# S5 mixer of a hybrid decoder trunk: from a scan over 256 tokens to chunks of 8 tokens

## The reference, cut to what matters

```python
xr = jnp.einsum('blgh,gph->lbgp', ug, bbr)
xi = jnp.einsum('blgh,gph->lbgp', ug, bbi)
# h[t] = a * h[t-1] + x[t], complex, over the 256 positions
_, _, hr, hi = lax.associative_scan(_complex_linear_combine, (ar.., ai.., xr, xi), axis=0)
y = (jnp.einsum('lbgp,ghp->blgh', hr, c_re) - jnp.einsum('lbgp,ghp->blgh', hi, c_im) + d * ug)
y = jax.nn.gelu(y.reshape(bsz, seq, B_WIDTH))
y = y * jax.nn.sigmoid(y @ glu_w + glu_b)
```

## Time and profile before

| | us |
|---|---|
| median of 3 runs (lowest, highest) | 800.15 (800.11, 800.49) |
| profiled execution, its own time | 800.82 |
| its span | 798.8 |
| TensorE busy | 687.8 (86%) |
| VectorE busy | 524.1 (66%) |
| ScalarE busy | 362.2 (45%) |
| GpSimd busy | 316.4 (40%) |

### The profile page before, as it was taken

One profiled execution on the slowest core, in us unless ns is written; L12 is line 12 of the kernel. 1 busy time (PEld: TensorE's weight loads), 2 busy tenths in 40 slices (PEclk: granted clock), 3 DMA queues, 4 the chain that ended last, 5 costly groups with the idle time before them and its releaser, 6 DMA issues.

```text
span 798.8 us, 11006 instructions
## 1 busy us (share of the span) xinstructions
PE 687.8 (86%) x4020; PEld 606.3 (76%) x4020; DVE 524.1 (66%) x925; ACT 362.2 (45%) x656; POOL 316.4 (40%) x485
## 2 busy tenths in 40 slices
PE   2881944988989999999999697597998999999994
PEld 2771833976879999999978585476788999999983
DVE  5629999486385555666557999768447645555553
ACT  3550142366554454444436316155735544444441
POOL 5699993255305349999000444335510000000000
PEclk9995885799999999999999988689999999999998
DMA  9530310010168556556635350000125566666631
GB/s 258 172 105 0 111 52 1 1 53 27 54 185 246 196 186 185 167 184 201 210 108 169 105 163 1 1 27 27 54 89 166 167 203 191 187 185 188 186 127 80
DMA packets 51876, 100.25 MB, mean 126 GB/s; under 512 B 11093, under 2 KB 15902, under 8 KB 51822
## 3 DMA queue, kind: packets, MB, share of 16 engines
q1 hardware_dynamic: 48750, 96.40, 39.0%
q0 software_dynamic: 720, 1.97, 1.0%
q10 hardware_dynamic: 2352, 1.18, 0.6%
HBM read 98.48 MB, written 1.05 MB: 125 GB/s over the span
## 4 chain that ended last, share of the span: by engine, by line
PE 61%; DVE 25%; issue 6%; POOL 4%; ACT 2%; DMA 1%; DVEq 0%; SPq 0%; ACTq 0%; POOLq 0%
PE pb L1408 61%; DVE dtmp L978 6%; DVE w_lo L1051 4%; DVE scan L1119 2%; DVE dtmp L985 1%; DVE x L985 1%; DVE btab L1320 1%; POOL e L519 1%; DVE h_lo L985 1%; POOL bt L519 1%; DMA pos_i<-in_positions 1%; DVE top L1204 1%; DVE scan L978 1%; ACT btab L884 1%; DVE dtmp L1109 1%
## 5 line engine op out<-in xcount | busy, mean ns | idle before, releaser
L1051 DVE TENSOR_TENSOR w_lo<-raw,w_hi 128x1024 fp32r<-128x1024 f32 (+2 forms) x176 | 220.1, 1268 | 140.5 <-ACT w_hi L725 140.2
L725 ACT ACTIVATE w_hi<-raw 128x1024 fp32r<-128x1024 f32 (+2 forms) x184 | 188.2, 1028 | 255.0 <-PE pb L1408 255.0
L1408 PE MATMUL pb<-h_hi,w_hi 128*128 128x256 f32 x512 | 145.0, 283 | 1.8 <-DVE h_lo L985 1.8
L1408 PE MATMUL pb<-h_lo,w_hi 128*128 128x256 f32 x512 | 144.9, 283 | 0.0
L1408 PE MATMUL pb<-h_hi,w_lo 128*128 128x256 f32 x512 | 144.9, 283 | 0.0
L523 POOL TENSOR_SCALAR pst<-stat 128x2 f32<-128x2 f32 (+1 forms) x11 | 2.8, 255 | 307.5 <-ACT proj L729 278.7
L1408 PE MATMUL pb<-w_hi,h_hi 128*128 128x512 f32 (+2 forms) x224 | 86.0, 384 | 21.3 <-DVE w_lo L1051 20.4
L1408 PEld LDWEIGHTS pb<-h_hi,w_hi 128*128 128x128 f32 x512 | 98.2, 192 | 2.7 <-DVE w_lo L1051 2.2
L1408 PE MATMUL pb<-w_hi,z_hi 128*128 128x512 f32 x256 | 99.8, 390 | 0.0
L1408 PE MATMUL pb<-w_hi,z_lo 128*128 128x512 f32 x256 | 99.8, 390 | 0.0
L1408 PE MATMUL pb<-w_lo,z_hi 128*128 128x512 f32 x256 | 99.6, 389 | 0.0
(11 more groups left out here) (267 smaller groups left out, 1212.2 us busy)
## 6 DMA issues: line engine op xcount, KB each, us to landing
raw<-in_w_up SPq DMA_DIRECT2D x64, 512.0 KB, 3.8
raw<-in_w_down SPq DMA_DIRECT2D x64, 512.0 KB, 4.3
raw<-in_w_in SPq DMA_DIRECT2D x24, 512.0 KB, 4.6
raw<-in_w_out SPq DMA_DIRECT2D x16, 512.0 KB, 3.8
raw<-in_w_in SPq DMA_DIRECT2D x8, 308.0 KB, 3.1
raw<-in_w_in SPq DMA_DIRECT2D x8, 280.0 KB, 3.2
x<-in_x ACTq DMA_DIRECT2D x1, 1024.0 KB, 5.3
out<-x SPq DMA_DIRECT2D x2, 512.0 KB, 2.7
```

Source lines behind the costliest of these rows:

```text
L725: hi_made.by(act.activation(w_hi[:, n % RING, 0:width(n)], raw[:, n % RING, 0:width(n)], ACT.Copy))
L1051: lo_made.by(dve.tensor_tensor(w_lo[:, n % RING, 0:width(n)], raw[:, n % RING, 0:width(n)], w_hi[:, n % RING, 0:width(n)].bitcast(F32), AL ...
L1408: return pe.matmul(o, l, r, start=start, stop=stop, skip_group_check=True)
```

## The change

The sequence is cut into 32 chunks of 8 tokens, and a chunk's work becomes products.

- `uc`: eight transfers take u from rows of tokens to rows of chunks (SP, after piece 10), ScalarE reorders it, TensorE transposes it to `uu` (16 inputs times 8 tokens on the partitions, 32 chunks along them).
- `bp`: GpSimd forms B times a power of the state factor for each place in the chunk; 16 transposes give `sw`. `s5_sums`, 32 products, gives what each chunk adds to the states.
- `s5_states` on VectorE turns these by `rot`, runs one scan over 32 chunks of all eight pairs for each of the two parts, turns back, and writes the state at each chunk's start to `ez`.
- `s5_kernel`, 16 products of B with `ca` (C times a power), gives the response at lags 0 to 7. `s5_lags` adds the D term and copies to `rk`. SP writes `rk` to memory and reads it back in 16 transfers as the triangular blocks `tk`.
- `s5_out` is 16 products of `tk` with `uu` and 16 of `ca` with `ez`. The result has rows of channel and place in the chunk. After the GELU it is transposed (`y_back`), regrouped by eight transfers to `ytok`, and transposed again (`y_turned`) for the GLU product, which moves to unit 14; ScalarE's first two `split` parts move from units 15 and 17 to 17 and 18.
- The four rounds, `et`, `btab`, `ctab` and GpSimd's turning back are gone. C is loaded by SP for both layers and laid out by ScalarE (`c_table`), for layer 1 during layer 0.
- In layer 0 TensorE's first transposes wait for x itself instead of a mark of VectorE; VectorE clears `bd`, `ez` and `tk` at the start and sums `ident` to `m16`.

```diff
-ROUNDS = 4
+CQ = 8
+NC = SEQ // CQ
...
+                        if n == 11:
+                            sp.wait_ge(tile_sb.sem, tile_sb.at(L, 1))
+                            for t in range(TT):
+                                for q in range(4):
+                                    sp.dma_start(uc[32 * q + 16 * t:32 * q + 16 * t + 16],
+                                                 proj[:, t, O_U + 64 * q:O_U + 64 * q + 64]).then_inc(uc_in.sem, 16)
+                        if n == 16 and L < DEPTH - 1:
+                            sp.wait_ge(ct_ps.sem, ct_ps.at(L, 1))
+                            load_c(sp, L + 1)
...
+                        if n == 24:
+                            sp.wait_ge(rk_sb.sem, rk_sb.at(L, 1))
+                            sp.dma_start(rk_hbm[L], rk).then_inc(rk_out.sem, 16)
+                            sp.wait_ge(rk_out.sem, rk_out.at(L, 16))
+                            rows = rk_hbm[L].rearrange("(g i) j n -> i j g n", i=16)
+                            for s in range(CQ):
+                                for j in range(2):
+                                    sp.dma_start(tk[16 * s:16 * s + 16, 8 * j:8 * j + 8, s:CQ, :].rearrange("p g s o -> p g (s o)"),
+                                                 rows[:, j, :, 0:PART - 16 * s]).then_inc(tk_in.sem, 8 * 2)
+                        if n == 26:
+                            sp.wait_ge(yb_sb.sem, yb_sb.at(L, 1))
+                            for t in range(TT):
+                                for g in range(4):
+                                    sp.dma_start(ytok[:, t, 64 * g:64 * g + 64],
+                                                 yc[32 * g + 16 * t:32 * g + 16 * t + 16].rearrange("p s q o -> p s (q o)"))\
+                                        .then_inc(yt_in.sem, 16)
...
+                for g in range(2):
+                    m = pool.tensor_copy(bd[64 * g:64 * g + 64, :, :, g, :], bb[64 * g:64 * g + 64])
+                    if g == 0:
...
+                pool.wait_ge(prep_b.sem, prep_b.at(occ, 1))
...
+            def prep_inputs(occ):
...
+                step(pool.tensor_copy(pmag[:, :, 1], S(1)))
...
+                for n in (1, 2, 4):
+                    tt(pmag[:, :, n + 1:2 * n + 1], pmag[:, :, 1:n + 1],
+                       pmag[:, :, n:n + 1].to_broadcast([PART, PAIRS, n]), ALU.mult, False)
+                    step(double(pw, n, n))
+                for i in range(2):
+                    tt(pa[:, i], pw[:, i], pmag[:], ALU.mult, i == 1)
+                A = [pa[:, i, :, CQ:0:-1].unsqueeze(3).to_broadcast([PART, PAIRS, CQ, 16]) for i in range(2)]
+                B = [bb[:, i].unsqueeze(2).to_broadcast([PART, PAIRS, CQ, 16]) for i in range(2)]
+                prep_w.by(cmul(bp[:, :, 0], bp[:, :, 1], A[0], A[1], B[0], B[1], *W))
...
+            def prep_outputs(occ):
+                step(pool.tensor_copy(dec[:, :, 1:NC], pmag[:, :, CQ:CQ + 1].to_broadcast([PART, PAIRS, NC - 1])))
+                pool.wait_ge(prep_w.sem, prep_w.at(occ, 1))
...
                 for n in (1, 2, 4, 8):
...
+                    step(double(rot, n, n))
+                prep_r.by(double(rot, 16, 15))
+                pool.wait_ge(prep_r.sem, prep_r.at(occ, 1))
...
+                tt(ca[:, :, 0], A[0], B[0], ALU.mult, False)
+                tt(W[0], A[1], B[1], ALU.mult, False)
+                tt(ca[:, :, 1], A[0], B[1], ALU.mult, False)
+                tt(W[1], A[1], B[0], ALU.mult)
+                tt(ca[:, :, 0], ca[:, :, 0], W[0], ALU.add, False)
+                prep_c.by(pool.tensor_tensor(ca[:, :, 1], ca[:, :, 1], W[1], ALU.subtract))
...
-                for r in range(ROUNDS):
-                    pool.wait_ge(scanned.sem, scanned.at(L, r + 1))
...
+                if L == 0:
+                    prep_outputs(0)
...
+                    if n == 12:
+                        act.wait_ge(uc_in.sem, uc_in.at(L, 16 * 8))
+                        uc_sb.by(act.activation(up_.rearrange("p l (s h) -> p l s h", s=CQ),
+                                                uc.rearrange("p s (l h) -> p l s h", l=4), ACT.Copy))
+                act.wait_ge(u_ps.sem, u_ps.at(L, 1))
+                u_sb.by(act.activation(uu[:].rearrange("p (q l) c -> p l q c", l=4),
+                                       pb[0][:].rearrange("p (l q c) -> p l q c", l=4, q=4), ACT.Copy))
...
+                act.wait_ge(sw_ps.sem, sw_ps.at(L, 1))
+                for i, b in enumerate((1, 2, 3, 0)):
...
+                sw_sb.by(m)
...
-                    if i in (4, 6):
-                        transposed(6 + (i - 4) // 2)
+                    if i in (2, 5):
+                        transposed(6 + (i - 2) // 3)
...
+                    if i == 4:
+                        act.wait_ge(y_ps.sem, y_ps.at(L, 1))
+                        y_sq.by(act.activation(yt, pb[7][:], ACT.Square, scale=0.044715 ** 0.5))
+                    if i == 6:
...
+                    if i == 9:
+                        act.wait_ge(yb_ps.sem, yb_ps.at(L, 1))
+                        yb_sb.by(act.activation(yc.rearrange("p s q o -> p q s o"),
+                                                pb[7][:].rearrange("p (q s o) -> p q s o", q=4, s=CQ), ACT.Copy))
+                    if i == 13:
+                        act.wait_ge(yk_ps.sem, yk_ps.at(L, 1))
+                        yk_sb.by(act.activation(yg, pb[7][:], ACT.Copy))
...
+                def s5_states():
+                    dve.wait_ge(xs_ps.sem, xs_ps.at(L, 1))
+                    dve.wait_ge(prep_r.sem, prep_r.at(L, 1))
...
+                    tt(P[0], x2, c2, ALU.mult, False)
+                    xs_read.by(dve.tensor_tensor(P[1], x2, s2, ALU.mult))
...
+                    dve.wait_ge(xs_read.sem, xs_read.at(L, 1))
+                    tt(P[2][:, 0], P[0][:, 0], P[1][:, 1], ALU.add, False)
+                    tt(P[2][:, 1], P[0][:, 1], P[1][:, 0], ALU.subtract)
...
+                    for i in range(2):
+                        step(dve.tensor_tensor_scan(P[3][:, i], d, P[2][:, i], 0.0, ALU.mult, ALU.add), i == 1)
+                    tt(P[0], P[3], c2, ALU.mult, False)
+                    tt(P[1], P[3], s2, ALU.mult)
...
+                    for g in range(2):
...
+                        step(dve.tensor_tensor(ez[h, 0, :, g, 1:NC], Q[0][h, 0], Q[1][h, 1], ALU.subtract), False)
+                        m = dve.tensor_tensor(ez[h, 1, :, g, 1:NC], Q[1][h, 0], Q[0][h, 1], ALU.add)
...
+                    ez_made.by(m)
...
+                def s5_lags():
+                    dve.wait_ge(rk_ps.sem, rk_ps.at(L, 1))
...
+                    step(dve.tensor_copy(rk[:, :, 16:PART], src[:, :, 16:PART]), False)
...
+                        m = stt(rk[:, j, 0:16], m16[:], s5d[:, L, j:j + 1], src[:, j, 0:16], ALU.mult, ALU.add)
...
+                    rk_sb.by(m)
...
-                for n in range(12, 16):
+                for n in range(12, 20):
...
+                def u_transposed():
+                    pe.wait_ge(uc_sb.sem, uc_sb.at(L, 1))
+                    for g in range(4):
+                        m = pe.transpose(pb[0][:, g * PART:(g + 1) * PART], up_[:, g, :], ident[:])
+                    u_ps.by(m)
...
+                def s5_inputs():
+                    pe.wait_ge(prep_w.sem, prep_w.at(L, 1))
+                    pe.wait_ge(u_sb.sem, u_sb.at(L, 1))
+                    if L == 0:
+                        pe.wait_ge(ct_sb.sem, ct_sb.at(0, 1))
+                    for j in range(PAIRS):
+                        for i in range(2):
+                            b = (1, 2, 3, 0)[j // 2]
+                            m = pe.transpose(pb[b][:, (2 * (j % 2) + i) * PART:(2 * (j % 2) + i + 1) * PART],
+                                             bp[:, j, i].rearrange("p s h -> p (s h)"), ident[:])
+                    sw_ps.by(m)
...
+                def s5_sums():
+                    pe.wait_ge(sw_sb.sem, sw_sb.at(L, 1))
+                    for i in range(2):
+                        for j in range(PAIRS):
+                            for g in range(2):
+                                m = mm(pb[2][64 * g:64 * g + 64, i * SEQ + j * NC:i * SEQ + (j + 1) * NC],
+                                       sw[:, j, i, 64 * g:64 * g + 64], uu[:, 2 * j + g, :], (i, j) == (0, 0), True)
+                    xs_ps.by(m)
...
+                def s5_kernel():
+                    pe.wait_ge(prep_c.sem, prep_c.at(L, 1))
...
+                        for i in range(2):
+                            for jj in range(4):
+                                j = 4 * a + jj
+                                m = mm(pb[7][32 * jj:32 * jj + 32, a * PART:(a + 1) * PART],
+                                       bd[:, i, j].rearrange("p g h -> p (g h)"),
+                                       ca[:, j, i].rearrange("p s h -> p (s h)"), (a, i) == (0, 0), i == 1)
+                    rk_ps.by(m)
...
+                tile(1)
                 tile(2)
-                bu(1)
+                u_transposed()
+                s5_inputs()
```

(39 more changed lines are left out.)

372 lines of the change are left out of this document (158 added, 214 removed).

## The result

Measured: 764.64 us median (761.49 to 766.20, 4 runs) against 800.32 (800.11 to 801.12, 4 runs), a ratio of 0.9548 with the 95% interval 0.9516 to 0.9579. The profiled execution took 766.2, its span 764.5. The forecast was 755, so the kernel is 36 us faster where 45 were expected. The time was gained where it was looked for, and more of it than forecast; a good part was given back in the attention loop.

The account below looks back on a forecast made before the run. The chain was TensorE 61% and VectorE 25%, the latter in two pre-loop stretches. From 800.82: -32.7 (layer 0), -15.7 (layer 1), +4 (loops), -0.4 (start) gave 756.0, median 755; range 741 to 777.

Parts of the forecast that it names:

- The gate of layer 0: Layer 0 before the loop: GpSimd's prep_w becomes the gate, bp at 58.5 (55 to 63), tile 3 starting at 61.5.
- forecast 17.9: From the end of tile 4 to the loop start, VectorE sets the time and takes 17.9 us in each layer.
- s5_sums is ... 64 records: Before tile 4: 32 float32 products, two records each, priced from c_first and other short products at 7.0 us.
- The upper end, 7.5: Upper end of the forecast's range for s5_sums, 7.0 us, with 3.5 as the lower end.
- Rival C: s5_sums products run in pairs on overlapping column groups: 3.5 us less per layer, 748 in all; chance 0.13.
- priced cold (13.1): Layer 0 before the loop: tile 3 takes 13.1 us, as an earlier tile 3 that also restarted cold.
- 64 records of 0.117, 7.5: In the attention loop: s5_out takes 7.5 us against 9.1 before, a gain of 1.6 a layer.
- rival A: Short products don't get the upper clock: s5_out costs 7.5 us more a layer, 770 or 776; chance 0.20.
- Priced 0.9: In the loop: tk lands at T+12.0, TensorE reaches s5_out at T+11, so it waits 0.9 us.
- Rival B: Transfers of rk and tk follow each other at landing time: 54 us more a layer, 861; chance 0.05.
- forecast hidden by 0.8: In the loop: y transfers land at 553.1, before unit 12 ends near 553.9, so they cost TensorE nothing.

Follow-up runs that it names:

- the run with the other order: Kernel after the change, with s5_sums and s5_kernel products ordered one output column group after another instead of alternating: 767.98 us, ratio 0.9601 to the kernel before.
- the run with early lags and exchanged operands: Kernel after the change, with s5_kernel and s5_lags earlier, tk read back in 8 transfers, and s5_out's operands exchanged: 746.06 us, ratio 0.9323 to the kernel before.
- the exchange alone: Kernel after the change, with s5_out's operands exchanged: uu and ez as weights, tk and ca moving, y_back gone: 743.56 us, ratio 0.9287 to the kernel before.

## Why the prediction was right or wrong

**Right: where the gain is.** The gate of layer 0 moved as worked out (`bp` written at 56.65, forecast 58.5; tile 3 at 60.85, forecast 61.5). There are no rounds, the ropes go at 0.2 to 0.4 us an operation once GpSimd is silent (450.21 to 452.95 for all three in layer 1, 2.7 against 3.2), `s5_states` took 6.3 against 6.2, and the eight operations of the index scores 2.9, as forecast. GpSimd beside it, up to 85.4, cost layer 0 its first ropes: from the end of tile 4 to the loop start 20.4, forecast 17.9; layer 1, without it, 17.0. That VectorE pays for GpSimd's work, an inference from the earlier trace rows, is now an experiment.

**Wrong, too dear: the short products ahead of the loop.** "s5_sums is ... 64 records", 7.0: it takes 2.06 in both layers. The step took the 7.04 of `c_first` as a price, but that row stands behind 9.71 us of idle time, and in the windows of before the first 12 us of the two loops have a clock of 0.54 and 0.50. Of the 5.0 us, 3.3 are the clock (7.0 to 3.7) and 1.65 the column groups (3.71 to 2.06), by the run with the other order. The upper end, 7.5, was the safe side; the lower one, 3.5, was not low enough. Rival C had a chance of 0.13 and was right in its mechanism. Tile 3 of layer 0 was priced cold (13.1), from a row that restarted after a wait; its own wait was 0.47, the transposes had come before, and it took 11.0.

**Wrong, too cheap: s5_out.** "64 records of 0.117, 7.5": 13.9 in each layer. That is rival A, with its price (7.5 a layer, measured 6.4) and its sign; it stood at 0.20 because the clock of before had risen 12 us into the loop. The products during which it rose there have 256 moving columns; these have 32 and 64. The forecast counted records and took the clock from the place in the program; in the runs it went with what stood there: full-width products in front gave 1.00, and the row of short ones stayed at 0.50 or fell to 0.52. The term is 12.8 us in all, more than the 10 by which the forecast was low.

**The sum had luck.** Up to the loops the kernel was better than forecast by 5.0 and 5.9, in the loops worse by 10.8 and 7.8, in the MLP worse by 2.7. Two large misses of opposite sign brought the time into the range.

**Mis-sized: the wait.** `tk` landed at T+12.8 and T+11.5, forecast T+12.0, round trip 2.9 and 1.4, issues 0.49 to 0.53. But TensorE came at T+8.6 and T+5.5, not T+11: in layer 1 the loop began at the upper clock and `c_first` took 3.9 instead of 7. Priced 0.9, it was 4.2 and 6.1; yet 2.1 us of each were not the transfers' but ScalarE's, in the same place. Rival B, the transfers one after the other, did not come (8 us for 16).

**Missed: the MLP of layer 0.** +2.7, forecast 0. From the first update to layer 1's first transposes it is 203.4 before and 206.1 after; in the traces of the experiments it is 204.8 in seven and 205.3 to 206.7 in four. So at least 1.4 stays in every run, and the other 1.3 of the profiled one goes with a window at a clock of 0.91 (200 to 220). A row shows the likely cause of half of the 1.4: the 1024-element products on GpSimd (2.8 to 3.4 us each) now hold VectorE's `w_lo` pieces, 6 of them in 13.05 us, and TensorE waits for `w_lo` three times there, 0.66 in all. An earlier stretch of the same kind (7 pieces in 19.5 us) cost TensorE nothing. No run undid it, so that is argued only, and the other 0.7 has no row.

```profile
333.55 13.05 DVE L1153 TENSOR_TENSOR w_lo<-raw,w_hi 128x1024 fp32r<-128x1024 f32 x6
336.65 0.36 PE L1489 MATMUL pb<-h_hi,w_hi 128*128 128x256 f32 x1 [0.30 <-DVE w_lo L1153]
```

The y transfers cost 0.4 in front of `y_turned` in each layer, forecast hidden by 0.8. What stays open is why the run with early lags and exchanged operands was no faster than the exchange alone: in its trace, the slowest of its four executions (750.78 against a median of 746.06), the clock fell again in other places of the loop (a mean of 0.50 over 4 us, some 72 us into that of layer 0), and what did that was not isolated.

## What to carry to other kernels

A duration of a short product is a price only together with the granted clock of its window: read both, and ask what kind of product the new row is, because long rows of products with 32 or 64 moving columns ran here at half clock while the engine was never idle. Turn such products so that the short side is the weights and consecutive ones write different groups of output partitions; the same sums took 2.8 to 4.4 us instead of 13.9. And before pricing a wait, look what stands behind it: here a removed wait of 4 to 6 us was worth 2 to 4, and moving one thing earlier paid nothing clear of the noise until all that fed the same point was moved together.

## What the runs showed of the hardware

- The granted clock stayed at 0.50 over 14.0 us of unbroken short float32 products (0.22 us a record), and fell from 1.00 to 0.52 within such a row that had begun at 1.00; full-width products in front gave 0.114 a record at once, and ten more between the halves kept it at 0.114 to the end.
- Float32 records with 64 weight columns: 32 ns when two column groups alternate, 58 in one. With 32 weight columns and 128 moving: 30 to 34 ns in four groups, 76 in one (all at the upper clock).
- VectorE beside GpSimd: six updates of 128 and 256 elements 7.14 us, alone 2.31.
- Sixteen small transfers on one queue: 0.49 to 0.53 us an issue, the last landing 1.3 to 1.5 us after its issue; eight of twice the size: 0.47 to 0.65 an issue in the ten loops of the five runs that have them.
